# Attention of a two-block network: four sequences per layer, one for each pair of heads, become one sequence per layer, and the local query norm moves into the softmax

## The reference, cut to what matters

```
z = q @ k.T * scale                                   # stick-breaking, s < t only
w = exp(log_sigmoid(z) + sum over s<j<t of -softplus(z_tj))
o_sb = w @ v

q = apply_rope(rms_norm_2(sw_q, q_norm_g), cos, sin)  # window attention
k = apply_rope(rms_norm_2(sw_k, k_norm_g), cos, sin)
scores = q @ k_band.T * scale                         # keys t-128 < s <= t
probs = softmax([scores, sink])[..., :-1]
o_swa = probs @ v_band

x = x + (g0 * (o_sb @ w_branch_sb) + g1 * (o_swa @ w_branch_swa)) @ w_out
x = x + relu(h2 @ w_up)**2 @ w_down
```

## Time and profile before

| | |
|---|---|
| median of three runs | 2786.04 us (2785.56 to 2786.64) |
| the profiled execution, its own time | 2787.14 us |
| its span, first to last instruction | 2785.7 us |
| PE busy | 2710.9 us, 97% of the span |
| DVE busy | 1533.3 us, 55% |
| ACT busy | 1173.1 us, 42% |
| POOL busy | 166.7 us, 6% |
| mean granted TensorE clock | 0.993 |

### The profile page before, as it was taken

One profiled execution on the slowest core, in us unless ns is written; L12 is line 12 of the kernel. 1 busy time (PEld: TensorE's weight loads), 2 busy tenths in 40 slices (PEclk: granted clock), 3 DMA queues, 4 the chain that ended last, 5 costly groups with the idle time before them and its releaser, 6 DMA issues.

```text
span 2785.7 us, 31002 instructions
## 1 busy us (share of the span) xinstructions
PE 2710.9 (97%) x12494; PEld 2188.9 (79%) x12494; DVE 1533.3 (55%) x2063; ACT 1173.1 (42%) x1702; POOL 166.7 (6%) x143
## 2 busy tenths in 40 slices
PE   8999999999999999999999999999999999999998
PEld 6888878888887888886666888888866668888887
DVE  4666657465687747476445554443554545544443
ACT  6444344243475424254545333332444553333322
POOL 2333110000010000000110000000001000000000
PEclk9999999999999999999999999999999999999999
DMA  4111113323333332332111232223221112222322
GB/s 170 53 57 57 52 59 106 98 89 101 106 99 103 98 98 99 99 106 76 46 38 46 91 98 92 97 98 99 98 68 39 46 46 99 91 98 94 99 95 76
DMA packets 66670, 235.55 MB, mean 85 GB/s; under 512 B 7520, under 2 KB 8032, under 8 KB 66528
## 3 DMA queue, kind: packets, MB, share of 16 engines
q1 hardware_dynamic: 63504, 228.58, 24.9%
q10 hardware_dynamic: 3024, 4.99, 0.6%
HBM read 231.44 MB, written 2.10 MB: 84 GB/s over the span
## 4 chain that ended last, share of the span: by engine, by line
PE 84%; ACT 7%; DVE 6%; issue 2%; POOL 1%; DMA 0%; SPq 0%; ACTq 0%; DVEq 0%
PE bank L411 25%; PE bank L413 25%; PE bank L412 25%; ACT w_hi_k L892 1%; DVE w_lo_k L1393 1%; PE bank L762 1%; PE bank L822 1%; ACT p_t_att L1300 1%; PE bank L801 1%; ACT L899 1%; DVE st_att L1862 1%; PE bank L753 1%; PE bank L814 1%; POOL q_mix L2000 1%; PE bank L746 0%
## 5 line engine op out<-in xcount | busy, mean ns | idle before, releaser
L411 PE MATMUL bank<-x_hi_k,w_hi_k 128*128 128x512 f32 x2152 | 868.4, 404 | 11.8 <-DVE x_lo_k L1400 10.8
L892 ACT ACTIVATE w_hi_k<-raw_k 128x1024 fp32r<-128x1024 f32 x431 | 454.5, 1058 | 937.7 <-PE bank L413 936.3
L413 PE MATMUL bank<-x_hi_k,w_lo_k 128*128 128x512 f32 x2152 | 842.9, 392 | 0.0
L412 PE MATMUL bank<-x_lo_k,w_hi_k 128*128 128x512 f32 x2152 | 842.7, 392 | 0.0
L1393 DVE TENSOR_TENSOR w_lo_k<-raw_k,w_hi_k 128x1024 fp32r<-128x1024 f32 x431 | 532.7, 1236 | 179.0 <-ACT w_hi_k L892 179.0
L411 PEld LDWEIGHTS bank<-x_hi_k,w_hi_k 128*128 128x128 f32 x2152 | 407.7, 189 | 107.9 <-issue 15.1
L413 PEld LDWEIGHTS bank<-x_hi_k,w_lo_k 128*128 128x128 f32 x2152 | 406.5, 189 | 87.3
L412 PEld LDWEIGHTS bank<-x_lo_k,w_hi_k 128*128 128x128 f32 x2152 | 407.3, 189 | 82.2 <-issue 4.1
L411 PE MATMUL bank<-y_hi_k,w_hi_k 128*128 128x512 f32 x1136 | 445.5, 392 | 3.2 <-DVE y_lo_k L1726 1.9
L413 PE MATMUL bank<-y_hi_k,w_lo_k 128*128 128x512 f32 x1136 | 442.9, 390 | 0.0
L412 PE MATMUL bank<-y_lo_k,w_hi_k 128*128 128x512 f32 x1136 | 442.7, 390 | 0.0
(11 more groups left out here) (315 smaller groups left out, 2544.2 us busy)
## 6 DMA issues: line engine op xcount, KB each, us to landing
raw_k<-wstream SPq DMA_DIRECT2D x431, 512.0 KB, 3.3
outT<-h_k ACTq DMA_DIRECT2D x8, 256.0 KB, 2.9
h_k<-xT SPq DMA_DIRECT2D x4, 256.0 KB, 8.3
h_k<-xT ACTq DMA_DIRECT2D x4, 256.0 KB, 7.7
decay_mix<-constants ACTq DMA_DIRECT2D x4, 256.0 KB, 2.6
levels_mix<-constants SPq DMA_DIRECT2D x1, 448.0 KB, 11.0
vec_k<-vectors SPq DMA_DIRECT2D x1, 282.5 KB, 9.6
cos_mix<-constants SPq DMA_DIRECT2D x1, 256.0 KB, 10.2
```

The lines of the kernel that those rows point to most:

```text
L411: pe.matmul(dst, wh, rh, start=start, stop=False)
L412: pe.matmul(dst, wh, rl, start=False, stop=False)
L413: return pe.matmul(dst, wl, rh, start=False, stop=stop)
L892: act.activation(k.w_hi[:, u % SPLIT, :], k.raw[:, u % RAW, :], ACT.Copy).then_inc(*hi_done.mark())
```

## The change

It rewrites how attention is ordered and moves one norm.

1. `beside_pairs` replaces `between_pairs`: one list of 21 units (84 parts) runs beside a whole layer. The last unit of pair 0, the window queries, moves from before the sequence to its head.
2. Stick-breaking is one task over the layer's 32 tiles, in 35 rounds of three slots. In round g, slot 0 makes the output of tile g-3 (and transposes the next pair's values), slot 1 transposes tile g-2, slot 2 makes the logits of tile g. On DVE the scan of tile g-1 is in slot 0 of round g, on ACT the copy of the transposes of g-2 in slot 1 and the sigmoids of g in slot 2.
3. The window task is one task of 106 slots. Pair m starts at slot 24 m. Relative to that: queries on DVE in 6 to 8, squares in 7, sums in 9, scores in 10 and 22, maxima in 11 and 23, root in 12, offsets in 13 and 23, exponentials in 13 and 25, division in 15 and 27, transposes in 17 and 29, outputs in 19 and 31.
4. The query norm: `wq` holds gain times query, rotated, without the root. The sums are made turned, four products of `sq` (as weights) with two columns of the matrix of halves, so a 128x8 result in a corner of bank 3. The root of that, `rq`, has one value for a token and head. It multiplies the maxima on DVE and is the per-partition scale of the exponentials on ACT. One table load of ln/exp serves the root and the first head's exponentials; a load of sigmoid follows each head's exponentials.
5. The keys' norm and rotation move from before the sequence to DVE's first four slots. Scan, copies and counts of the stick tiles stay as they were.

Steps that share a slot come in the order stick, then window. Where the computed points of the two differ in the last binary digit it can be the other way round: with these numbers that is so in slots 12, 25, 34, 36, 38, 51, 64, 68, 69, 72, 73, 77, 78 and 103. Fill part k (from 0) lies at slot (k+1) * 106/84 - 1.

```diff
+def beside_pairs(layer):
+    units = [("pair", layer, 0, 3)]
+    units += [("pair", layer, pair, n) for pair in (1, 2) for n in range(4)]
+    units += [("merge", layer, 0, 0)]
+    units += [("pair", layer, 3, n) for n in range(4)]
+    return units + [("merge", layer, m, gate) for m in range(KEPT_GATES) for gate in range(2)][1:]
...
+STICK_LAG = 3
+STICK_SLOTS = 3 * (ALL_TILES + STICK_LAG)
+PAIR_SLOTS = 3 * TILES
+HALF_AT = (10, 22)
+WINDOW_SLOTS = PAIR_SLOTS * (PAIRS - 1) + HALF_AT[1] + 12
...
+def layer_tasks(stick, window, fill):
+    return ((stick, STICK_SLOTS, 0, STICK_SLOTS / WINDOW_SLOTS), (window, WINDOW_SLOTS, 0, 1),
+            (filling(fill, len(fill.units) * PARTS), len(fill.units) * PARTS, 0, 1))
...
+        for g in range(ALL_TILES + STICK_LAG):
+            if g >= 3:
+                output(g - 3)
+            if g >= 2 and (g - 2) % TILES == 0 and g - 2 < ALL_TILES:
+                values((g - 2) // TILES)
             yield
+            if 2 <= g < ALL_TILES + 2:
+                turned(g - 2)
             yield
+            if g < ALL_TILES:
+                logits(g)
+            yield
...
+            for n in range(TC):
+                mm = pe.matmul(wq_sums(k)[:, n, :], ch(k.sq, n), k.halves[:, 0:P:64], start=True, stop=True)
...
+            for n in range(TC):
+                act.activation(k.p_t[:, n, :], score_view(k, n), ACT.Exp, scale=k.rq[:, n, half:half + 1],
+                               bias=k.st[:, 1, n:n + 1], accum_out=k.st[:, 2, n:n + 1]).then_inc(*mark())
...
+                    if at == HALF_AT[half] + 2:
+                        ln_exp_tables()
+                        if half == 0:
+                            act.wait_ge(*pe_done.at("wq_sum", layer, m))
+                            inverse_root(k.rq[:], wq_sums(k), 1.0 / 64, "wq_root", layer, m)
+                    if at == HALF_AT[half] + 3:
+                        exps(m, half)
+                        sigmoid_tables()
```

More of the change, by code:

```diff
@@ L67 @@
 NSMALL = 3 * P
[L70 to L80, removed]
+PAIRS = 4
+def beside_pairs(layer):
[4 more added lines that the diff above has]
+    return units + [("merge", layer, m, gate) for m in range(KEPT_GATES) for gate in range(2)][1:]
 def unit_order():
@@ L100, in unit_order @@
         units += [("kv", layer, n) for n in range(2)]
-        units += [("pair", layer, 0, n) for n in FIRST_PAIR]
-        for pair in range(4):
-            units += between_pairs(layer, pair)
+        units += [("pair", layer, 0, n) for n in range(3)]
+        units += beside_pairs(layer)
         units += [("merge", layer, m, n) for m in range(KT) for n in range(2 if m < KEPT_GATES else 0, 3)]
@@ L135 @@
 for _layer in range(LAYERS2):
[L136 to L138 removed]
+    for _n in range(3):
+        BANK["pair", _layer, 0, _n] = (3, 4, 1)[_n]
+    for _n, _name in enumerate(beside_pairs(_layer)):
         BANK[_name] = _n % 2
@@ L789, in window, with sums, scores @@
+            yield
+    def window(layer):
+        def sums(m):
+            pe.wait_ge(*act_done.at("wq_sq", layer, m))
+            for n in range(TC):
+                mm = pe.matmul(wq_sums(k)[:, n, :], ch(k.sq, n), k.halves[:, 0:P:64], start=True, stop=True)
+            mm.then_inc(*mark("wq_sum", layer, m))
+        def scores(m, half):
             if half == 0:
-                pe.wait_ge(*dve_done.at("wq", *at))
-            else:
-                pe.wait_ge(*act_done.at("wo", *at, 0))
+                pe.wait_ge(*dve_done.at("wq", layer, m))
+            if half == 1 or m > 0:
+                pe.wait_ge(*act_done.at("wo", layer, m - 1 + half, 1 - half))
@@ L802, in window, with turned @@
                                    start=False, stop=True)
[L803 to L810, removed]
+            mm.then_inc(*mark("scores", layer, m, half))
+        def turned(m, half):
+            pe.wait_ge(*dve_done.at("probs", layer, m, half))
             for n in range(TC):
@@ L823, in window @@
                                start=n == 0, stop=n == 3, skip_group_check=True)
-            mm.then_inc(*mark("wo", *at, half))
+            mm.then_inc(*mark("wo", layer, m, half))
+        for slot in window_slots():
+            for m, at in slot:
+                if at == HALF_AT[0] - 1:
+                    sums(m)
+                for half in range(2):
+                    if at == HALF_AT[half]:
+                        scores(m, half)
+                    if at == HALF_AT[half] + 7:
+                        turned(m, half)
+                    if at == HALF_AT[half] + 9:
+                        output(m, half)
             yield
@@ L830, in attention @@
              between=(lambda: sum_squares(bank[7][:], k.ssum, stage)) if layer == 1 else final_sums)
-        first = Fill([("pair", layer, 0, n) for n in FIRST_PAIR], fill_piece)
+        first = Fill([("pair", layer, 0, n) for n in range(3)], fill_piece)
         first.part(4)
@@ L841, in attention @@
         first.rest()
-        for pair in range(4):
-            interleave(*pair_tasks(stick(layer, pair), window(layer, pair), Fill(between_pairs(layer, pair), fill_piece)))
+        interleave(*layer_tasks(stick(layer), window(layer), Fill(beside_pairs(layer), fill_piece)))
     def merge(layer):
@@ L1335, in attention @@
         inverse_root(k.rstd[:], bank[6][:], 1.0 / 64, "wk_root", layer)
-        window_squares(layer, 0)
         first.rest()
-        for pair in range(4):
-            interleave(*pair_tasks(stick(layer, pair), window(layer, pair), Fill(between_pairs(layer, pair), fill_piece)))
+        interleave(*layer_tasks(stick(layer), window(layer), Fill(beside_pairs(layer), fill_piece)))
     def merge(layer):
@@ L1834, in rope @@
+    def rope(dst, rot, *event):
         for a in range(0, P, 64):
@@ L1903, in fill_piece @@
             w_low()
-        first = Fill([("kv", layer, n) for n in range(2)] + [("pair", layer, 0, n) for n in FIRST_PAIR], fill_piece)
+        first = Fill([("kv", layer, n) for n in range(2)] + [("pair", layer, 0, n) for n in range(3)], fill_piece)
         first.part(8)
@@ L1908, in attention @@
             h_final(range(KT))
-        first.part(4)
-        dve.wait_ge(*act_done.at("wk_root", layer))
-        dve.wait_ge(*now())
-        dve.scalar_tensor_tensor(k.wk[:], k.wk[:], vcol("k_gain2", layer), k.rstd[:], ALU.mult,
-                                 ALU.mult).then_inc(*mark())
-        first.part(4)
-        rope(k.wk, k.rot).then_inc(*mark())
-        dve.wait_ge(*now())
-        for half in range(2):
-            r, other = head_rows(half)
-            mm = dve.tensor_scalar(k.zwk[r, half, :], k.wk[r, :], 0.125, None, ALU.mult)
-            mm.then_inc(*(mark("wk", layer) if half else mark()))
+        first.part(8)
+        queries_and_keys(layer, 0)
         first.rest()
-        for pair in range(4):
-            interleave(*pair_tasks(stick(layer, pair), window(layer, pair), Fill(between_pairs(layer, pair), fill_piece)))
+        interleave(*layer_tasks(stick(layer), window(layer), Fill(beside_pairs(layer), fill_piece)))
     def merge(layer):
```

354 lines of the change are left out of this document (168 added, 186 removed).

## The result

The changed kernel takes 2791.2 us, the median of 15 runs (2788.5 to 2795.9), against 2786.0 for the kernel before (2785.6 to 2787.1). The ratio is 1.0022, with a 95% interval of 1.0014 to 1.0029: slower by 0.2%, where I had forecast 2763. Its runs spread over 7.5 us and those of before over 1.5. The spread goes with the clock: the fastest run, 2788.5, has a mean granted clock of 0.993 and the slowest, 2795.9, has 0.990. The profiled executions took 2795.0 us and, in the kernel before, 2787.1, so they lie 7.9 apart where the medians lie 5.1 apart.

A forecast was written before the change was run, and what follows sets the result against it. PE's products were taken as the bound, with idling and a lowered clock in attention. Terms -45.4 - 13.0 + 29.0 + 2.4 + 4.4 = -22.6 us on 2786.0 gave 2763 us, with 2725 to 2784 for 8 in 10.

The forecast's parts named there:

- Removed: PE's old waits in the two attention stages, 45.4 us idle plus 13 us of lowered clock, can go.
- The mechanism and the places: PE's window transposes wait for DVE's division, which stands behind table load, sigmoids and scan; 1.2 to 3.4 us each.
- Their size: PE's new waits on the window's division: 14.5 us a layer, 29.0 us in all.
- POOL beside the division: POOL multiplying as DVE's division starts: costs nothing, or up to 1.1 us more at 12 places, 13 us.
- The start: At each layer's start, with DVE doing the keys within the sequence, PE waits 1.2 us: 2.4 in all.
- The stick chain at nothing: Stick-breaking from logits to transposes to output: both steps hidden behind PE's other work, costing nothing.
- The clock: Of the new waits only four come near 3.9 us; two clock falls at 2.2 us: 4.4, ends 0 and 9.
- The norm at nothing: The query norm's eight sums become four small products each: 3 us gained to 3 lost, taken as nothing.
- A: The window's division is hidden after all and only the layer start costs 2.4 us: 2730 us, chance 0.23.
- B: ACT's queue makes each of 14 divisions wait 3.3 us with a 2.2 us clock fall: 2807 us, chance 0.10.
- C: Each table switch holds ACT about 1.3 us more, 12 waits grow by 16 us: 2784 us, chance 0.05.
- D: New waits at each tile as sigmoids wait behind the window's work, 64 tiles at 1 us: 2792, chance 0.04.

The follow-up runs named there:

- the experiment: Changed kernel with a constant scale and a constant offset column in the exponentials, leaving out query norm and maximum: 2782.1 us.
- all edits together: Changed kernel with the division in the exponentials' slot, stick first in every shared slot and the keys ahead of the sequence: 2730.9 us.

## Why the prediction was wrong, step by step

*Removed: 45.4 us of waits and 13 of clock.* Right, but for the copy's wait, of which 2.6 is left. The other old waits went, and the clock in the kernel before measures as 14.2, of which the trace puts 1.6 outside attention. What I did not see is that 6.6 of it can be had only with the queries' chain off the path, which this change also does.

*The mechanism and the places.* Right. I forecast one new wait, the division's, at seven places a layer, none at the eighth, longest in the first head of pair 0 and the second of pair 2. Two of the three longest are there; the longest of all, 4.13, is in the first head of pair 3. In layer 0, forecast and measured: 3.3 and 3.96; 1.8 and 1.35 (with 1.30 at an output just before); 1.3 and 1.97; 1.2 and 1.25; 1.7 and 2.51; 3.4 and 3.80; 1.8 and 4.13; 0 and 0.31.

*Their size: 29.0 forecast, 38.6 measured.* Three parts of the term were too small. The scale operand "taken as free" costs 0.09 us in each of 64 exponentials, 5.1 us of wait by the experiment. POOL beside the division, for which I took nothing and kept 13 as the end of the range, costs 8.0; my reason, that only operations with two inputs are held, was wrong: the one that stood has one tensor input. And at the first head of pair 3 I let the unit's end delay the exponentials by 0.5 only. The offsets stand on DVE in slot 85, behind the landing and low part at 84.81, so they wait with it:

```profile
1496.85 0.69 DVE L1936 SCALAR_TENSOR_TENSOR gates_att<-bank,scale_k 128x512 f32<-128x512 f32 x1 [2.93 <-PE bank L426]
1498.00 1.23 DVE L1406 TENSOR_TENSOR w_lo_k<-raw_k,w_hi_k 128x1024 fp32r<-128x1024 f32 x1 [0.46 <-ACT w_hi_k L912]
1499.14 0.15 DVE L1885 TENSOR_TENSOR st_att<-st_att,rq_att 128x4 f32<-128x4 f32 x1
...
1504.51 1.23 DVE L1830 TENSOR_TENSOR_SCAN kept_att<-keep_att,zeros_att 128x512 f32<-128x512 f32 x1 [4.95 <-ACT stick_w_att L1293]
```

The exponentials began at 1499.60, 1.4 us after ACT was free for them. These three exceed the 9.6 that was missing. What I had too high elsewhere takes the rest back, above all slot 25, where window comes first and the output waits 1.30 just before the division.

*The start: 2.4 forecast, 4.2 measured.* The count of DVE's operations was right (my terms add up to 16.9 us, not 17.2), but two of them ran beside POOL and took 1.19 and 1.48 us, where the shortest of their kind in the trace take 0.49 and 0.69. I had left POOL out of the price of the start. The second has two inputs and would have been held by my own assumption.

*The stick chain at nothing.* Right but for two output waits of 1.3, which come from ACT making the exponentials ahead of the copy in slot 25. I had the slot in my list and did not follow what stood behind it on ACT.

*The clock: 4.4 forecast, 14.6 measured by the medians, some 20 in the profiled execution.* The step that failed most. I let a wait bring the clock down only if it was near 3.9, since those of 1.7 had not. Between 1.7 and 3.9 the attention of before shows nothing, and I placed the boundary at its upper end. But I had looked at attention alone. Ahead of it, the trace of before has a wait of 1.85 and behind that the seventh stretch:

```profile
859.83 0.50 PE L411 MATMUL bank<-y_hi_k,w_hi_k 128*128 128x512 f32 x1 [1.85 <-DVE y_lo_k L1726]
860.00:864.00 4.00, 4.00 (x11) 3.17 (x12) 3.90 (x6) 2.83 (x4) 0.00 (x0) 0.57 0.22 71
```

In the changed kernel's trace all twelve waits in attention from 1.97 up brought the clock down, but the same wait of 1.85 ahead of attention did not. So the length of one wait does not decide it. With POOL behind the division, a wait of 3.15 left the clock at full speed:

```profile
2222.89 1.09 PE L822 MATMUL bank<-con_k,p_t_att 128*128 128x128 f32 x8 [3.15 <-DVE p_t_att L1897]
2220.00:2224.00 4.00, 1.11 (x9) 1.11 (x10) 3.86 (x10) 0.05 (x1) 1.02 (x1) 1.00 0.39 131
2224.00:2228.00 4.00, 4.00 (x20) 2.77 (x20) 2.48 (x3) 2.68 (x6) 1.17 (x2) 1.00 0.00 0
```

What decides between such waits stays open. That it differs from wait to wait fits with the spread: runs of kernels with such waits differ by 5 to 11 us, those with hardly any by 1 to 4, except that the kernel before, with its six, stays within 1.5 in the runs beside the changed kernel and within 3.8 in others.

*The norm at nothing.* Right: a set of sums takes 0.91 us instead of 0.86, eight of them 0.4.

The sum in the forecast's terms, for the two profiled executions: 38.6 + 4.2 + 2.6 + 0.4 = 45.8 of waits against 45.4 is 0.4 slower, the clock with an estimated 20.5 against 14.4 is 6.1, the sums are 0.4, and 1.3 comes from waits ahead of attention, where the slow stretch at 860 us had hidden one of 1.36. That makes 8.2 where 7.9 was measured. So the waits in attention came out even, and by this estimate the kernel is slower by its clock. The median lies 3.8 us below the profiled execution, with less of the clock's share, and so comes to 5.1.

*The rivals.* A (hidden division, 2730) did not happen here. With the division hidden by a move of its own (2738.5) 10 us of the waits at the start, at the outputs and on POOL are left; only all edits together reach A's time. B had the mechanism that came true, at some four fifths of its size: 14 waits of 2.7 on average where B had 3.3, with a clock fall at ten of them, and its point of decision, "from a mean wait of 1.8 us on with a fall each", was the right one. I gave it 0.10 on the ground that 1.7 us had left the clock up. C's dear table switch does not show: the load begins at 1321.86, takes 1.28 us, and keep begins at 1323.15, right behind its end. D did not happen. The range ended at 2784 because I let the costs that I had bounded (13 for POOL, 9 for the clock) add up only by half; together they are +17.6 on 2763, and with the 3 of the norm would have reached 2784 without the errors of place.

## What to carry to other kernels

When a long sequence is merged from tasks slot by slot, ask of each engine what stands directly ahead of the instruction that the bottleneck waits for, and place a step where its input is ready, not where its turn in the pattern is: moving one division by one slot was worth 50.7 us, ten times the change's own effect. Price an idle PE with its clock: on top of some 45 us of waits in attention came some 13 us of clock in the kernel before and 15 to 20 in the changed one, all of it beside waits of 1.97 us and more. Look for the shortest wait that the clock fell behind in the whole trace, not in the stage at hand. And where a slow clock follows a wait, expect that taking the wait away uncovers the next chain.

## What was not expected of the hardware

- A DVE TENSOR_SCALAR of 128x256 with one tensor input stood 1.02 us instead of 0.34 while POOL multiplied; only the first of four, to the end of POOL's operation.
- A column operand as scale adds 0.09 us to an ACTIVATE of 128x256 (0.563 against 0.474).
- Sums with two output columns are no cheaper than with 512. The first line is the new form and the next one starts 0.91 us later; the old one took 0.86 (1357.38 to 1358.24 in the kernel before).

```profile
1304.47 1.05 PE L797 MATMUL bank<-con_k,sq_k 128*128 128x2 f32 x8
1305.38 0.48 PE L424 MATMUL bank<-x_hi_k,w_hi_k 128*128 128x512 f32 x1
```

- In one execution the granted clock fell after all twelve waits of PE of 1.97 to 4.13 us in attention. In another kernel it did not after one of 3.15, and after the same wait of 1.85 it fell in one kernel and stayed in the other.
